# Gathers of four slots by 32 tokens, and value products on four 32-column quarters of the array

## What is computed

```python
def block(tb):
    q = (tb @ wq).reshape(P_BLOCK, P_HEADS, P_DKEY)
    s1 = jnp.einsum('thd,nd->thn', q[..., :half], k1)
    s2 = jnp.einsum('thd,nd->thn', q[..., half:], k2)
    v1, i1 = lax.top_k(s1, P_TOPK)
    v2, i2 = lax.top_k(s2, P_TOPK)
    cand = v1[..., :, None] + v2[..., None, :]          # 16 x 16 sums
    sc, pos = lax.top_k(cand, P_TOPK)                   # idx: the 16 experts
    g = jax.nn.softmax(sc, axis=-1)
    pre = jnp.einsum('td,thkd->thk', tb, u[idx])
    act = jax.nn.gelu(pre) * g
    return jnp.einsum('thk,thkd->td', act, v[idx])
```

## Time and profile before

| | us |
|---|---|
| median of three runs | 4762.41 |
| span of the profiled execution | 4754.3 |
| first dot of the gather loop (on DVE) starts at | 1800.52 |
| first dot of the last, small tile starts at | 4631.67 |
| PE busy in the span | 4255.9 (90%) |
| DVE busy in the span | 3116.5 (66%) |
| ACT busy in the span | 996.5 (21%) |
| gathers, from issue to landing (median in the loop) | 12.1 |

### The profile page before, as it was taken

One profiled execution on the slowest core, in us unless ns is written; L12 is line 12 of the kernel. 1 busy time (PEld: TensorE's weight loads), 2 busy tenths in 40 slices (PEclk: granted clock), 3 DMA queues, 4 the chain that ended last, 5 costly groups with the idle time before them and its releaser, 6 DMA issues.

```text
span 4754.3 us, 50461 instructions
## 1 busy us (share of the span) xinstructions
PE 4255.9 (90%) x16837; PEld 2643.1 (56%) x16837; DVE 3116.5 (66%) x7138; ACT 996.5 (21%) x2580; POOL 1481.0 (31%) x1391
## 2 busy tenths in 40 slices
PE   8999999999898889888888999778988888888878
PEld 8999777888765675445443555323433433434332
DVE  3444113666377538887789777677777777777784
ACT  2222111234266301110111111111212111212212
POOL 1100002222111003444444444444444444444442
PEclk8999999999899999999999999999999999999999
DMA  2223222344323359999999999999999999999996
GB/s 93 69 89 124 88 91 75 123 129 129 110 77 109 113 180 369 396 413 410 417 405 409 403 416 405 420 420 403 409 409 419 385 402 416 397 416 408 383 413 259
DMA packets 310425, 1379.14 MB, mean 290 GB/s; under 512 B 37856, under 2 KB 112336, under 8 KB 175024
## 3 DMA queue, kind: packets, MB, share of 16 engines
q0 software_dynamic: 167728, 1166.48, 60.6%
q1 hardware_dynamic: 142464, 209.70, 12.8%
HBM read 1295.58 MB, written 80.49 MB: 289 GB/s over the span
## 4 chain that ended last, share of the span: by engine, by line
PE 31%; DMA 19%; DVE 10%; issue 4%; POOL 1%; ACT 0%; DVEq 0%; ACTq 0%; POOLq 0%
DMA peer_uv<-in_peer_uv_dram,peer_idx 19%; PE peer_acc L2740 19%; PE peer_fo L2675 4%; PE peer_fo L2688 2%; PE peer_fo L2576 2%; DVE peer_uv L2000 2%; PE peer_tb L2520 2%; DVE peer_diag L2030 1%; DVE peer_hot L1958 1%; DVE peer_hot L1961 1%; POOL peer_uv L1864 1%; DVE peer_sel L1964 1%; PE peer_fo L2594 0%; PE peer_acc L2624 0%; DVE peer_pos L1948 0%
## 5 line engine op out<-in xcount | busy, mean ns | idle before, releaser
L2740 PE MATMUL peer_acc<-peer_uv,peer_diag 128*128 128x512 f32 (+1 forms) x4000 | 1932.3, 622 | 303.5 <-DVE peer_diag L2030 296.3
L1864 POOL DMA_INDIRECT peer_uv<-in_peer_uv_dram,peer_idx x1056 | 1232.5, 1167 | 1704.5 <-PE peer_acc L2740 1577.2
L2000 DVE CUSTOM_DVE_ANT_0 peer_uv<-peer_uv,peer_h 128x1024 f32<-128x1024 f32 x1056 | 1290.7, 1222 | 639.9 <-DMA peer_uv<-in_peer_uv_dram,peer_idx 637.7
L2740 PEld LDWEIGHTS peer_acc<-peer_uv,peer_diag 128*128 128x128 f32 (+1 forms) x4000 | 742.3, 195 | 1285.5 <-issue 727.3
L2479 ACT ACTIVATE peer_ge<-peer_pre 128x1 f32<-128x1 f32 x1056 | 212.8, 203 | 2425.7 <-DVE peer_pre L2000 2425.1
L2675 PE MATMUL peer_fo<-peer_space 128*128 128x256 f32 (+2 forms) x1152 | 395.6, 475 | 42.0 <-DVE peer_space L2094 16.9
L99 PE MATMUL proj_bank<-proj_hTh,proj_wplead 128*128 128x352 f32 x1008 | 357.7, 355 | 1.8 <-DVE proj_wprest L91 1.8
L2030 DVE TENSOR_SCALAR peer_diag<-ident,peer_ge,peer_gw 128x128 f32<-128x128 f32 x968 | 332.2, 343 | 9.7 <-ACT peer_ge L2479 7.4
L2675 PEld LDWEIGHTS peer_fo<-peer_space 128*128 128x128 f32 x1152 | 221.7, 197 | 204.9 <-issue 157.8
L100 PE MATMUL proj_bank<-proj_hTr,proj_wplead 128*128 128x352 f32 x1008 | 328.8, 326 | 0.0
L101 PE MATMUL proj_bank<-proj_hTh,proj_wprest 128*128 128x352 f32 x1008 | 328.6, 326 | 0.0
(11 more groups left out here) (370 smaller groups left out, 5418.0 us busy)
## 6 DMA issues: line engine op xcount, KB each, us to landing
proj_wp<-in_w_in_dram POOLq DMA_DIRECT2D x13, 2048.0 KB, 9.8
peer_space<-in_w_ssm_o_dram SPq DMA_DIRECT2D x48, 512.0 KB, 7.6
peer_uv<-in_peer_uv_dram,peer_idx POOLq DMA_INDIRECT x1056, 12.1
proj_wp<-in_w_in_dram POOLq DMA_DIRECT2D x14, 1024.0 KB, 8.3
peer_space<-in_w_attn_o_dram SPq DMA_DIRECT2D x24, 512.0 KB, 7.9
peer_space<-in_w_out_dram SPq DMA_DIRECT2D x24, 512.0 KB, 7.8
scratch_xtok<-proj_shared SPq DMA_DIRECT2D x20, 512.0 KB, 3.2
scratch_chan<-proj_stg SPq DMA_DIRECT2D x48, 176.0 KB, 1.8
```

The costliest lines, as they stand in the source:

```text
L1864: pool.indirect_dma_start(uv[k][:], None, io["peer_uv"], bass.IndirectOffsetOnAxis(ap=idx[t % 2][:, col:col + 1], axis=0)).then_inc(uv_in[ ...
L2000: dve.tensor_tensor_reduce(uv[k][:, 0:D], uv[k][:, 0:D], h2[t % 2][:], 1.0, 0.0, ALU.mult, ALU.add, pre[g % 2][:, k:k + 1]).then_inc(u_don ...
L2740: x = pe.matmul(acc[0:r, h:h + HALF], diag[k][:, 0:r], uv[k][:, D + h:D + h + HALF], start=(it == 0 and k == 0), stop=False)
```

## The change

A gather now holds four slots of 32 tokens: partition 32c+m of gather j of a quad is token 32j+m with slot 4a+c. Four gathers (`QUAD`) together are four slots of all 128 tokens, and the bytes are the same as before. What follows from it:

- **Indices and weights** are written by quarter of the partitions: `placed` and `taken_from` turn one write of 32 columns on 128 partitions into 16 writes of 8 columns on 32 partitions, for `idx` and for `gw`.
- **h2 copies.** The dot needs the 32 tokens of its gather in all four quarters. PE makes, by `replicate`, four copies `rep[j]` a tile, in quarters of the array, and ACT copies them out (`rep_copy`).
- **Weights** once a quad: GELU for four columns at once, `both` = GELU times `gw`, and `scaled`, four 128x32 matrices, in one DVE instruction each. They stand after the first dot of the next quad.
- **Value products** once a quad: eight matmuls of 512 columns with a 128x32 weight, gather j into partitions 32j to 32j+31 of `acc`. `v_done` counts up once for a quad, and four buffers come free with it.
- The adding on DVE (`add_aside`) and the copying for the last tile (`place_copies`) go. The last tile still works by single gathers.
- To make room `h2` has one buffer, `s12` holds half the heads (its second half is filled later), and `x1` shares the buffer of `hT`, so it is loaded late in its tile.

```diff
+    QUAD = P // DEC
-    PE_AHEAD, POOL_BEHIND = 3, 7
+    PE_AHEAD, POOL_BEHIND = 3, 5
-    KEPT = 2
+    KEPT = 1
+    def handled(n):
+        return n // QUAD + 1 if n < WHOLE else WHOLE // QUAD + n - WHOLE + 1
 def fetch(t, g, it, k):
     if n >= SLOTS:
-        if aside(n - SLOTS):
-            pool.wait_ge(aside_done, asides[n - SLOTS])
-        else:
-            pool.wait_ge(v_done, products(n - SLOTS))
+        pool.wait_ge(v_done, handled(n - SLOTS))
 def choose(t, p, part):
-    dve.scalar_tensor_tensor(out=idx[t % 2][:, 2 * p * PTOP:(2 * p + 2) * PTOP]...,
-                             in0=sel[:, :, 0, :], scalar=float(PNK), in1=sel[:, :, 1, :],
-                             op0=ALU.mult, op1=ALU.add).then_inc(tk, 1)
+    for j, copy in quarters(t):
+        x = dve.scalar_tensor_tensor(out=placed(idx, t, p, j, copy), in0=taken_from(sel[:, :, 0, :], j, copy), scalar=float(PNK),
+                                     in1=taken_from(sel[:, :, 1, :], j, copy), op0=ALU.mult, op1=ALU.add)
+    x.then_inc(tk, 1)
 def weigh(t, p):
-    dve.tensor_tensor(gw[t % 2][:, 2 * p * PTOP:(2 * p + 2) * PTOP]..., ex[:],
-                      rtot[:].unsqueeze(2).broadcast_to([P, 2, PTOP]), ALU.mult).then_inc(weighed, 1)
+    for j, copy in quarters(t):
+        x = dve.tensor_tensor(placed(gw, t, p, j, copy), taken_from(ex[:], j, copy),
+                              rtot[quarter(j), :].unsqueeze(2).broadcast_to([DEC, 2, PTOP // QUAD]), ALU.mult)
+    x.then_inc(weighed, 1)
-def weights(t, g, it, k):
-    dve.tensor_scalar(diag[k][:, 0:r], c.ident[:] if r == P else fold[:], ge[g % 2][:, k:k + 1],
-                      gw[t % 2][:, it * SLOTS + k:it * SLOTS + k + 1], ALU.mult, ALU.mult).then_inc(diag_done, 1)
+def weights(n):
+    if n >= 2 * QUAD:
+        dve.wait_ge(v_done, handled(n - 2 * QUAD))
+    if t < LAST:
+        dve.wait_ge(gelu_done, handled(n))
+        dve.tensor_tensor(both[:], ge[q % 2][:], gw[t % 2][:, col - QUAD + 1:col + 1], ALU.mult).then_inc(both_done, 1)
+        dve.wait_ge(both_done, q + 1)
+        dve.tensor_tensor(scaled[q % 2][:], fold[:].unsqueeze(1).broadcast_to([P, QUAD, DEC]),
+                          both[:].unsqueeze(2).broadcast_to([P, QUAD, DEC]), ALU.mult).then_inc(scaled_done, 1)
 def slot(n):
     dots(t, g, k)
-    if n:
-        weights(*places[n - 1])
+    if n > WHOLE or n and n % QUAD == 0:
+        weights(n - 1)
+def rep_copy(t, j):                      # ACT
+    act.wait_ge(rep_made, n + 1)
+    if t:
+        act.wait_ge(u_done, t * PSLOT - QUAD + j + 1)
+    for h, place in enumerate(rep_place(t, j)):
+        x = act.activation(rep[j][:, h * HALF:(h + 1) * HALF], place, ACT.Copy)
+    x.then_inc(rep_out, 1)
+def replicate(t, j):                     # PE
+    for h, place in enumerate(rep_place(t, j)):
+        for copy in range(QUAD):
+            x = pe.matmul(place[copy * DEC:(copy + 1) * DEC, :], c.ident[:, j * DEC:(j + 1) * DEC],
+                          h2[:, h * HALF:(h + 1) * HALF], start=True, stop=True)
+    x.then_inc(rep_made, 1)
+def values(n, g, it, k):                 # PE
+    pe.wait_ge(scaled_done, handled(n))
+    for j in range(QUAD):
+        pe.wait_ge(uv_in[k - QUAD + 1 + j], g * 16 + 16)
+    for h in range(0, D, HALF):
+        for j in range(QUAD):
+            x = pe.matmul(acc[j * DEC:(j + 1) * DEC, h:h + HALF], scaled[n // QUAD % 2][:, j, :],
+                          uv[k - QUAD + 1 + j][:, D + h:D + h + HALF], start=(it == 0 and k == QUAD - 1), stop=False)
+    x.then_inc(v_done, 1)
```

More of the change, by code:

```diff
@@ L1692, in h2_ready @@
             else:
[L1693 removed]
+                eng.wait_ge(h2_in, 16 * (t - KEPT + 1))
         def source(t):
@@ L1705, in load_h2 @@
                     sp.wait_ge(h2_stored, h2_stores(group_of(t)))
-                    for copy in range(0, P, r):
-                        sp.dma_start(h2[t % 2][copy:copy + r, :], dr["h2"][tokens(t, r), :]).then_inc(h2_in[t % 2], 16)
+                    sp.wait_ge(rep_made, QUAD * t)
+                    sp.dma_start(h2[0:r, :], dr["h2"][tokens(t, r), :]).then_inc(h2_in, 16)
                 def load_x1(t):
@@ L1901, in _, with quarter, quarters, placed @@
                 dve.tensor_scalar(gall[:, 0:CB], gsub[:].broadcast_to([P, CB]), 1.0 - LAM_INIT, None, ALU.mult).then_inc(gains, 1)
+                def quarter(j):
+                    return slice(j * DEC, (j + 1) * DEC)
+                def quarters(t):
+                    return [(j, copy) for j in range(copies_of(t)) for copy in range(QUAD)]
+                def placed(x, t, p, j, copy):
+                    n = PTOP // QUAD * 2 * copies_of(t)
+                    return x[t % 2][quarter(copy), p * n:(p + 1) * n].rearrange("r (e a j) -> r e a j", e=2, j=copies_of(t))[:, :, :, j]
+                def taken_from(x, j, copy):
+                    return x[quarter(j)].rearrange("r e (a c) -> r e a c", c=QUAD)[:, :, :, copy]
                 def choose(t, p, part):
```

206 lines of the change are left out of this document (111 added, 95 removed).

## The result

The changed kernel takes 5435.2 us (median of 4 runs, 5427.9 to 5443.2) against 4762.4 for the kernel before: 1.142 times as long, interval 1.140 to 1.143. The forecast was 4910 us in a range of 4700 to 5150. The direction is right, the size is not: 673 us were lost where 150 were expected.

A forecast was written before the change was run, and what follows sets the result against it. DMA was taken to bound the loop. 4754.3 + 164 (tiles 3 to 7) - 23 (tiles 0 to 2) + 8 (start) = 4903 us; with the runs' median 8 us higher, 4910 us, range 4700 to 5150.

The forecast's parts named there:

- What bounds the loop: Gather loop before the change: DMA bounds it, PE holds it up in short stretches; relief of PE brings at most 94 us.
- The cushion: Return of gather buffers: 7.9 us to spare before the change, 0.2 us after it, when four buffers come back together.
- the larger of a chain and 10.0 us: Period of a quad: dot, matrices, burst, issue and landing, 9.8 us at the upper clock, against 10.0 for the next quad's landing.
- Tiles 0 to 2: Tiles with mixing beside them: upper PE clock, 1095 us against 1118, so -23 us.
- the ring: Cycle of eight gather buffers from landing through dot and value products to reissue and landing; its return chain after the change 9.8 us.
- Tiles 3 to 7: Late tiles: 375 us each, the middle of 360 at the upper and 391 at the lower PE clock; +164 us.
- lower case: Late tiles with PE at its lower clock: burst 3.7 us, chain 11.5, 391 us a tile.
- The quarters run together: Value burst on PE: four array quarters work side by side, 16 records in 2.0 us, 3.7 at the lower clock.
- the serial case: Rival for the value burst: quarters run one by one, burst 7.2 us, chain 15.0, 5800 us in all; chance 0.12.
- The start and the last tile: Copying matmuls ahead of the first dot add 8 us; the last tile, with single gathers, 0, give or take 3.
- What would show it: Signs in tiles 3 to 7: DMA share below 0.95, gather waits over 5 us, landings 6 to 9, PE under 60%, clock under 0.85.
- cold and crowded: Rival for the whole loop: lower clock everywhere, 6.5 us to land, 408 us a tile, 5195 us; chance 0.15.

The follow-up runs named there:

- bare_ring_half: Changed kernel without the choice of tokens and weights for tiles 4 to 8, and with half of the value products of tiles 0 to 7 left out: 5137 us.
- six_deep: Kernel before with at most six gathers outstanding in place of eight, buffers coming back one at a time, GpSimd's mixing 5 behind: 5081 us.
- before_by_fours: Kernel before, but a gather waits for the products of all four gathers of its buffer's group; GpSimd's mixing 5 gathers behind, not 7: 5229 us.
- values_first: Changed kernel with the value products of four gathers put ahead of the mixing and next-tile pieces in TensorE's slot: 5341 us.
- one_write: Changed kernel with the 16 small writes of token numbers and 16 of weights per pair of heads each replaced by one write (last tile excepted): 5322 us.
- bare_ring: Changed kernel with the choice of tokens and their weights for tiles 4 to 8 left out: 5290 us.
- one_quarter: Changed kernel with the products of all four gathers written to one array quarter, except each tile's first burst, so they can't run together: 6400 us.
- weights_early: Changed kernel with the weights of four gathers made right behind the fourth gather's own dot, not behind the next four's first dot: 5038 us.
- half_burst: Changed kernel with half of the value products of tiles 0 to 7 left out, except each tile's first burst: 5286 us.

## Why the prediction was right in direction and wrong in size

**What bounds the loop: right, as far as tried.** DMA bounds the kernel before, and relief of PE inside its loop brings little: before_half took half of the value products away and brought 33 us, under the 94 that were the limit.

**The cushion: the step that failed.** The forecast called the 6.4 us between a landing of 12.1 us and one of 5.7 queueing, "work that lies ready for DMA", 7.9 us to spare, and took the period to be the larger of a chain and 10.0 us. The whole sum of the loop rests on that. Two terms of it fail. The landing: the 5.7 us came from one gather with nothing queued. Behind a group that is still landing it was 6.8 in the turn shown, 6.5 on the mean of those turns of tiles 3 to 7 that waited for it, and 7.5 in bare_ring_half. That ring's chain would be 9.6 us with 5.7 in it, so by the larger of the two its turn would be 10.0; it is 11.5. And the way to the issue: in the kernel before, from a dot to the issue into its buffer took 8.7 us on the mean of tiles 3 to 7, where the chain has 6.4, so the spare time was 5.6 us at most and not 7.9. Nor was it free: six_deep takes 5.0 us and costs 322. What the release by fours costs by itself, in the kernel before, is 467 us.

**Tiles 0 to 2: -23 forecast, +291 measured, the largest miss.** The forecast's chain is 1.8 us to the burst, 2.0 the burst, 0.26 and 5.7; the mean turn has 3.7, 3.0, 0.4 and 7.7. The clock was to be the upper one, since PE stays busy; it was 0.77. before_by_fours shows 143 us for the ring, values_first 99 for the burst that stands behind a waiting piece of mixing, one_write 36 for the small writes; that is 278 of 291, but three edits to different kernels need not add up. The wait for the piece of mixing, 1.9 us a turn, was put at nothing in the prediction ("mixing on DVE adds some us to a border" is another thing): PE's order shows it, in which the products of a quad's first three gathers, too, now stand behind the mixing of its last slot.

**Tiles 3 to 7: +164 forecast, +383 measured.** The lower clock was right for these tiles, 0.66, and taking the middle of the two clocks cost 78 us: by the prediction's own lower case they are 5 x 391 = 1955 us. Of the remaining 142, some 90 are the ring without any choice, 12.0 us a turn in bare_ring where the lower case has 11.5, and some 50 the choice, 1.0 us a turn where it has 0.65: a part 4 took 7.2 us, from 4099.8 to 4107.0, where the sum has 5.9. The small writes showed 0.18 us each where 0.1 was taken. All of them together cost 82 us in these tiles (2097 against 2015 in one_write), of which the sum already had 64, 1.6 us twice in each of 20 pairs. That they cost more than the 0.1 us each is a small part of the miss.

**The quarters run together: right.** 16 records in 3.64 us at the lower clock and 1.92 at the upper, against 3.7 and 2.0 predicted; one_quarter excludes the serial case. The change from full-size matmuls to a burst, which the prediction couldn't price, shows in the timeline at the upper clock as 0.52 us from start to start, where two full matmuls of 512 columns are 0.43 apart, and the same on the way back: some 0.1 us each way.

**The start and the last tile: right.** First dot at 1807.8 against 1800.5, 7 us for 8; last tile -1 (121.4 us from its first dot to the end, for 122.6).

**What would show it.** All signs came: DMA share 0.87, waits for gathers over 5 us and 1353 us in sum, landings of 8.7 us, PE busy 41%, clock 0.66, four records starting together, the longest turns behind part 4 (16.6 us on the mean of tiles 3 to 7). They hold for a loss of any size: none of them had a size by which 4910 could be told from 5435. The case "cold and crowded", 5195 us, was the nearest and had 0.15. It had the lower clock and, with 6.5 us, the landing right, and its 408 us a late tile are near the 419 measured; its tiles 0 to 2 last 1224 us and not 1409, since it lacks the wait for mixing too.

**The sum of the parts as measured:** release by fours 467, small writes 113, the burst behind mixing 94; together 674 of 673 us. That the sum comes out is luck. The parts overlap, and were taken in different kernels: weights_early alone gives back 397 of the 673 us with the release by fours in place. What PE's relief gives back is not told apart in this, nor what the lower clock takes, but for half_burst's bound of some 150 us.
